# Fifteen of 32 experts in 64 rows with raw fp32 weights: one kernel for a transformer block with experts and a second block

## What is computed

```
def expert_block(args):
    xblk, e = args
    gu = xblk @ w_gate_up[e] + b_gate_up[e]
    gate = jnp.minimum(gu[:, :D_EXPERT], SWIGLU_LIMIT)
    up = jnp.clip(gu[:, D_EXPERT:], -SWIGLU_LIMIT, SWIGLU_LIMIT)
    act = gate * jax.nn.sigmoid(SWIGLU_ALPHA * gate) * (up + 1)
    return act @ w_down[e] + b_down[e]
```

## Time and profile before

| what | value |
|---|---|
| median of 3 runs | 1837.42 us (1836.15 to 1837.75) |
| the profiled execution's own time | 1836.11 us |
| its span | 1834.4 us |
| PE busy | 1756.2 us (96%) |
| DVE busy | 1517.9 us (83%) |
| ACT busy | 1148.2 us (63%) |
| POOL busy | 306.4 us (17%) |
| moved by DMA | 504.74 MB, 275 GB/s over the span |
| granted PE clock, mean | 0.98 |

### The profile page before, as it was taken

One profiled execution on the slowest core, in us unless ns is written; L12 is line 12 of the kernel. 1 busy time (PEld: TensorE's weight loads), 2 busy tenths in 40 slices (PEclk: granted clock), 3 DMA queues, 4 the chain that ended last, 5 costly groups with the idle time before them and its releaser, 6 DMA issues. The chain is left out here.

```text
span 1834.4 us, 25163 instructions
## 1 busy us (share of the span) xinstructions
PE 1756.2 (96%) x8429; PEld 1380.3 (75%) x8430; DVE 1517.9 (83%) x1693; ACT 1148.2 (63%) x1251; POOL 306.4 (17%) x331
## 2 busy tenths in 40 slices
PE   6988979999999999999999999999999799998998
PEld 3555457888888888888888888888886368887996
DVE  5366658999999999999999999999998657897663
ACT  5343316777777777777777777777774644436541
POOL 0140210121121121111112111111135100004420
PEclk9998969999999999999999999999999899999999
DMA  6032839999999999999999999999997522211001
GB/s 212 11 111 89 332 108 351 400 398 382 390 390 380 384 397 378 383 396 381 383 393 388 376 387 398 378 381 396 383 381 271 183 88 69 92 47 70 1 24 46
DMA packets 108519, 504.74 MB, mean 275 GB/s; under 512 B 22593, under 2 KB 40622, under 8 KB 58194
## 3 DMA queue, kind: packets, MB, share of 16 engines
q1 hardware_dynamic: 97314, 477.96, 67.6%
q0 software_dynamic: 11152, 26.10, 4.1%
HBM read 481.06 MB, written 22.95 MB: 275 GB/s over the span
## 5 line engine op out<-in xcount | busy, mean ns | idle before, releaser
L1776 DVE TENSOR_TENSOR part<-ring,part 128x2048 fp32r<-128x2048 f32 x258 | 584.4, 2286 | 35.5 <-ACT part L1474 35.5
L1474 ACT ACTIVATE part<-ring 128x2048 fp32r<-128x2048 f32 x256 | 486.4, 1921 | 135.2 <-PE bank L1627 75.4
L1604 PE MATMUL bank<-part,xT_hi 128*128 128x512 f32 x1536 | 390.8, 396 | 0.0
L1604 PEld LDWEIGHTS bank<-part,xT_hi 128*128 128x128 f32 x1536 | 281.4, 188 | 62.0 <-issue 7.3
L1474 ACT ACTIVATE part<-rest 128x2048 fp32r<-128x2048 f32 x124 | 238.2, 1922 | 96.4 <-PE bank L1604 70.9
L1776 DVE TENSOR_TENSOR part<-rest,part 128x2048 fp32r<-128x2048 f32 x124 | 281.3, 2292 | 0.0
L1638 PE MATMUL bank<-part,actT_hi 128*128 128x512 f32 x1024 | 277.0, 392 | 1.1 <-DVE part L1776 0.8
L1933 POOL DMA_INDIRECT rest<-h_rows,rest x33 | 88.1, 2671 | 944.9 <-PE bank L1587 928.6
L1638 PEld LDWEIGHTS bank<-part,actT_hi 128*128 128x128 f32 x1024 | 189.8, 188 | 39.5 <-issue 1.2
L1604 PE MATMUL bank<-part,xT_lo 128*128 128x512 f32 x768 | 205.9, 390 | 0.0
L1604 PEld LDWEIGHTS bank<-part,xT_lo 128*128 128x128 f32 x768 | 144.2, 188 | 31.4
(11 more groups left out here) (501 smaller groups left out, 2540.1 us busy)
## 6 DMA issues: line engine op xcount, KB each, us to landing
ring<-in_w_gate_up SPq DMA_DIRECT2D x194, 1024.0 KB, 7.8
ring<-in_w_down SPq DMA_DIRECT2D x66, 1024.0 KB, 6.8
rest<-in_w_gate_up SPq DMA_DIRECT2D x62, 1024.0 KB, 8.3
rest<-in_w_down SPq DMA_DIRECT2D x62, 1024.0 KB, 7.3
expert_rows<-rest SPq DMA_DIRECT2D x31, 512.0 KB, 8.4
ring<-in_w_in SPq DMA_DIRECT2D x14, 1024.0 KB, 5.2
rest<-in_w_ada SPq DMA_DIRECT2D x8, 1536.0 KB, 7.1
ring<-in_w_out SPq DMA_DIRECT2D x16, 512.0 KB, 5.9
```

The lines of the kernel that those rows point to most:

```text
L1474: nc.scalar.activation(hi[part(i, c)], raw(i, c), ACT.Copy).then_inc(sig("hi_ready"), counts)
L1604: ins = nc.tensor.matmul(bank[g][:], rows[:, c, :], w[:, g * 512:(g + 1) * 512], start=first, stop=last, skip_group_check=True)
L1776: V.tensor_tensor(lo[part(i, c)], raw(i, c), hi[part(i, c)].bitcast(F32), ALU.subtract).then_inc(sig("lo_ready"), counts)
```

## The change

The experts 1 to 30 are ranked by their number of rows when the router is done. The 15 with fewest take the odd turns ("small"), the other 15 the even turns ("big"); expert 0 stays first and 31 last. A small expert is computed for 64 rows. Its gathered rows are laid out in two halves: the partitions 0 to 63 hold the first half of the columns and 64 to 127 the second (`gather_small`, by rows of half the length). PE reads its raw fp32 chunks straight from the slots, with plain fp32 matmuls of 64 rows, two at a time by design: one writes to the partitions 0 to 63 of a bank, the other to 64 to 127 (the two column tiles). No high and low parts are made for it. Its activation is one 128 x 512 tile in place of two. Its slots come free when PE has used the chunk (`raw_used`). In a pair j, PE does gate and up of small expert j, down of the big one before, gate and up of the big one, down of the small one. The expert numbers are read by each engine from a table `order` that the first block makes; ranks, table and places of the results take new operations on DVE and three small matmuls on PE. An expert of the 15 with more than 64 rows would get an extra block.

The two projections use column tiles as well: the key rope's eight matmuls write to four groups of 32 partitions, and a matmul with `fold` adds them; the index keys' eight write to two groups of 64.

The diff, cut to its core:

```diff
+SMALL = 64
+PAIRS = 15
...
-            project(bank[4][64:96, :], w_in, D_IN1 - ROPE, ROPE)
+            for k in range(KT):
+                part = bank[4][32 * (k % 4):32 * (k % 4) + 32, :]
+                ins = nc.tensor.matmul(part, w_in[:, k, D_IN1 - ROPE:D_IN1], hT[:, k, :], start=(k < 4), stop=(k >= 4), skip_group_check=True)
+            ins.then_inc(sig("proj_done"), 1)
...
-            nc.tensor.matmul(bank[5][64:96, :], swap[64:96, :], k_rope[64:96, :], start=True, stop=True).then_inc(sig("k_swapped"), 1)
+            nc.tensor.matmul(bank[4][64:96, :], fold, k_rope, start=True, stop=True)
+            nc.tensor.matmul(bank[5][64:96, :], swap, k_rope, start=True, stop=True).then_inc(sig("k_swapped"), 1)
...
+            pe.wait_ge(sig("order_terms"), 1)
+            for n, by in enumerate((con(m, "token", 1, E - 1).broadcast_to([E - 1, P]), ones[0:E - 1, :], ones[0:E - 1, :])):
+                ins = nc.tensor.matmul(order_sum[:, n * E:(n + 1) * E], by, terms[0:E - 1, n * E:(n + 1) * E], start=True, stop=True, skip_group_check=True)
+            ins.then_inc(sig("ordered"), 1)
...
+            chain.link(V.scalar_tensor_tensor(out=key_row[0:E], in0=con(m, "iota", E, E), scalar=1.0 / 64, in1=count[0:E], op0=ALU.mult, op1=ALU.add))
+            chain.link(V.scalar_tensor_tensor(out=key_col[0:E], in0=con(m, "token", 1, E), scalar=1.0 / 64, in1=count_col, op0=ALU.mult, op1=ALU.add))
+            chain.link(V.tensor_scalar(under[0:E, 1:E - 1], key_row[0:E, 1:E - 1], key_col[0:E], 2.0, ALU.is_lt, ALU.mult))
+            chain.link(V.tensor_reduce(rank[0:E], under[0:E, 1:E - 1], AX, ALU.add))
...
+            dve.wait_ge(sig("ordered"), 1)
+            V.tensor_copy(f["order"][0:1], order_sum[0:1, 0:E])
...
+            chain.link(V.tensor_tensor(count[:, 1:E], count[:, 1:E], shift[:, 1:E], ALU.add))
             chain.link(V.tensor_scalar(extra, count, float(P), None, ALU.is_gt))
...
+            def store_small(j):
+                sp.wait_ge(sig("y_ready"), 2 * j + 4)
+                for g in range(2):
+                    sp.dma_start(m["y_dram"][bass.ds((P + SMALL) * j + P, SMALL), g * 512:(g + 1) * 512], y[g * SMALL:(g + 1) * SMALL, 0:512]).then_inc(sig("y_small_stored"), 16)
...
+            def rest_of_small(j, e, before):
                 for c in range(SLOTS, CHUNKS):
-                    wait_lo(sp, i, c - SLOTS)
-                    load_chunk(sp, a, m, i if c < 8 else i - 1, c, c % SLOTS)
+                    wait_raw(sp, j, c - SLOTS)
+                    load_chunk(sp, a, m, e if c < 8 else before, c, c % SLOTS)
...
+            with sp.Fori(0, PAIRS - 1) as j:
+                e1, e2 = (expert_at(sp, 2 * j + n) for n in (1, 2))
+                rest_of_big(j, e2, e1)
+                e3 = expert_at(sp, 2 * j + 3)
+                after_big(j, e3)
+                rest_of_small(j + 1, e3, e2)
+                after_small(j + 1, expert_at(sp, 2 * j + 4))
...
+            def gate_up_small(c, u):
+
+                w = raw_slot(m, c % SLOTS)
+                for h in range(2):
+                    ins = nc.tensor.matmul(bank[2 * u][h * SMALL:(h + 1) * SMALL, :], xT_small[:, c, :], w[:, (2 * u + h) * 512:(2 * u + h + 1) * 512], start=(c == 0), stop=(c == 7), skip_group_check=True)
+                return ins
...
+            def down_small(j, c):
+
+                pe.wait_ge(sig(f"chunk_loaded{c}"), 32 * j + 32)
+                w = raw_slot(m, c % SLOTS).rearrange("p (k n) -> p k n", k=2)
+                for k in range(2):
+                    n = 2 * (c - 8) + k
+                    for g in range(2):
+                        ins = nc.tensor.matmul(bank[6][g * SMALL:(g + 1) * SMALL, :], actT_small[:, n, :], w[:, k, g * 512:(g + 1) * 512], start=(n == 0), stop=(n == 7), skip_group_check=True)
+                ins.then_inc(sig("raw_used"), 1)
...
+            with pe.Fori(0, PAIRS - 1) as j:
+
+                small_turn(j)
+                big_gate_ups(j)
+                turn_rows_small(2 * j + 3)
+                pe.wait_ge(sig("index_ready"), 2 * j + 5)
+                big_down(j)
...
-            tile(1, w_small, 0, DI)
+            for k in range(KT):
+                ins = M.matmul(bank[1][64 * (k % 2):64 * (k % 2) + 64, :], w_small[:, k, 0:DI], hT[:, k, :], start=(k < 2), stop=(k >= KT - 2), skip_group_check=True)
+            ins.then_inc(sig("tile_done"), 1)
...
+            pe.wait_ge(sig("ik_parts_ready"), 1)
+            pe.wait_ge(sig("fold_ready"), 1)
+            M.matmul(bank[1][:], fold, ik_parts, start=True, stop=True).then_inc(sig("ik_folded"), 1)
```

More of the change, by code:

```diff
@@ L345, in first_block @@
     gsum, ginv = room.take(T), room.take(T)
+    key_row, under, terms = room.take(E), room.take(E), room.take(3 * E)
+    key_col, rank, small_e, at_e = (room.take(1) for _ in range(4))
+    order_sum = bank[4][:, (T + 2) * E:(T + 5) * E]
+    count_col = bank[4][0:E, (T + 1) * E:(T + 1) * E + 1]
     SCALE = QK ** -0.5
@@ L1285, in expert_places @@
     f["gate"], f["sigm"], f["up"], f["act"] = (keep.take(2, 512) for _ in range(4))
+    f["iota_small"], f["half"] = keep.take(P), keep.take(1)
     assert keep.at <= m["late_end"]
@@ new lines, in rest_of_big, with after_small @@
+            def rest_of_big(j, e, before):
+                for c in range(SLOTS, CHUNKS):
+                    wait_lo(sp, first(j) + 4 + c - SLOTS)
+                    load_chunk(sp, a, m, e if c < 8 else before, c, c % SLOTS)
+            def after_small(j, e, store=True):
+                for c in range(SLOTS):
+                    if c + SLOTS < 8:
+                        wait_raw(sp, j, c + SLOTS)
+                    else:
+                        wait_lo(sp, first(j) + c + SLOTS - 8)
+                    load_chunk(sp, a, m, e, c, c)
+                    if c == 0 and store:
+                        store_small(j - 1)
@@ L1529, in _ @@
-            make_hi(1, 3, 2, (0, 7))
-            make_hi(1, 4, 2, (0, 4))
-            make_hi(1, 5, 2, (0, 5))
-            with act.Fori(1, E - 1) as i:
-                turn(i)
-            i = E - 1
+            make_hi(2, 6 % RAW, "chunk_loaded6", 1, 2)
+            make_hi(3, 7 % RAW, "chunk_loaded7", 1, 3, counts=1 + 4)
+            sigmoid(7)
+            copy_rows_small(1)
+            with act.Fori(0, PAIRS - 1) as j:
+                small_turn(j)
+                for s in range(8, CHUNKS):
+                    hi_of_pair(j, s)
+                sigmoid(first(j) + 11)
+                copy_rows_small(2 * j + 3)
+                copy_y_small(j)
@@ L1536, in _ @@
+            j = PAIRS - 1
+            small_turn(j)
+            for s in range(8, CHUNKS):
+                hi_of_pair(j, s)
+            hi_of_last(0)
+            sigmoid(first(j) + 11)
+            hi_of_last(1)
+            copy_rows(E - 1, PAIRS + 2)
+            for c in (2, 3, 4):
+                hi_of_last(c)
+            copy_y_small(j)
+            hi_of_last(5)
             nc.scalar.activation(spare[0:1, 0:1], con(m, "ident", 1)[0:1], ACT.Sigmoid)
             for c in (6, 7):
-                make_hi(i, c, i + 1, (i, c - PARTS))
@@ L1704, in _ @@
-            i = E - 1
-            for h in range(2):
-                pe.wait_ge(sig(f"clipped{h}"), i)
-            gate_ups(i, i, more=False)
-            wait_actT(i)
-            pe.wait_ge(sig("y_ready"), i + 1)
+            first_gate_ups(0, (0, 1), 1)
+            for c in (2, 3):
+                gate_up(c, c, c)
+            biases(0)
+            gate_up(4, 4, 4)
+            list_next(0)
+            gate_up(5, 5, 5)
+            gate_up(6, 2, 6)
+            gate_up(7, 3, 7, counts=1 + 4)
@@ L1710, in _ @@
+            first_gate_ups(LAST, (0, 1), PAIRS + 2, [(f"act_ready{h}", PAIRS + 1) for h in range(2)])
+            turn_act(0, PAIRS + 1)
+            turn_act(1, PAIRS + 1)
+            for c in (2, 3):
+                gate_up(LAST + c, c, c)
+            biases(E - 1)
+            for c in (4, 5, 6, 7):
+                gate_up(LAST + c, c % PARTS, c)
+            wait_actT(PAIRS + 1)
+            pe.wait_ge(sig("y_ready"), E)
             for c in (8, 9, 10):
-                down(i, c)
+                down(LAST + c, c % PARTS, c)
@@ L1855, in _ @@
+            list_of(iota, expert_at(dve, 2))
+            index(2)
+            clip(7)
             gated(0)
-            rows_lo(2)
             times_gate(0)
+            with dve.Fori(0, PAIRS - 1) as j:
+                small_turn(j)
+                list_of(iota, expert_at(dve, 2 * j + 4))
+                for s in (6, 7, 8):
+                    lo_of_pair(j, s)
+                index(2 * j + 4)
+                for s in (9, 10, 11):
+                    lo_of_pair(j, s)
+                clip(first(j) + 11)
+                gated(j + 1)
+                times_gate(j + 1)
@@ L1858, in _ @@
+            j = PAIRS - 1
+            small_turn(j, last=True)
+            for s in range(6, CHUNKS):
+                lo_of_pair(j, s)
+            clip(first(j) + 11)
+            lo_of_last(0)
```

(9 more changed lines are left out.)

581 lines of the change are left out of this document (356 added, 225 removed).

## The result

The changed kernel takes **1846.57 us** (median of 5 runs, 1843.58 to 1849.50) against 1837.42 on the same chip: 1.005 times the kernel before, interval 1.0037 to 1.0063. It is 0.5% slower where I forecast 5% faster. The profiled execution took 1843.58 us, 1841.9 of it span.

What follows compares the result with a forecast made beforehand. PE bounds the loop now, DMA after the change; span 1834.4 - 90.9 + 3 + 3.4 - 2.3 - 3 = 1744.6 us, so 1746 us for an execution, about 5% faster, range 1708 to 1816.

Steps and rivals of the forecast that it cites:

- The view of the bound: Expert loop: PE sets the 35.33 us turn; after the change PE has 58.1 us a pair and DMA becomes the bound.
- Step 1: PE's small turn: 24 pairs of fp32 matmuls with column halves fully overlapping cost 21.0 us, replacing 32.6 us.
- rival B: Small gate-up and down on PE: column halves do not overlap, 79.1 us a pair, 1968 us; chance 0.10.
- C: Small turn on PE: halves overlap but weight loads do not, 71.3 us a pair, 1848 us; chance 0.03.
- Step 2: ACT and DVE in the loop: twelve copies and twelve subtractions a pair go; both then follow DMA, far under 60 us.
- step 3: DMA in the loop: mean 414 GB/s, 64.6 us a pair against 70.66, 90.9 us gained over fifteen pairs.
- PE's work at a low clock: After PE's idle at the end of each small gate-up: 1.5 to 2 us lost, covered by 6 us of slack.
- The mechanism that I gave for the thin queue: Big gate-ups: PE falls about 11 us behind DMA, small down chunks hold slots, queue thin for a quarter of the pair.
- Rival A: Loop: DMA cannot beat today's mean of 386 GB/s, 69.3 us a pair, 20 us gained, 1815 us; chance 0.12.
- Step 4: Order of experts: DVE waits for three small matmuls and does more operations before the first list, +3.4 us.
- Step 5: Projections in column tiles: key rope -2.3 us with two tiles at once, index keys -3 us.
- The last expert: Last expert: PE reaches its first two chunks while DMA is just ahead, about 3 us lost once.

Runs made afterwards that it cites:

- e11: e4 with both 64-row products of the small turn summed onto the same column half and bank half, so they cannot run side by side: 2002.73 us.
- e9: e4 without the loop's gathers of rows and gate-up bias loads, GpSimd signalling at once instead: 1757.94 us.
- e4: The changed kernel with the three moves of e1, e2 and e3 together: 1776.54 us, 0.9675 of the kernel before.
- e1: The changed kernel with DVE's copy of the big expert's index moved behind the last of the six subtractions: 1786.3 us.
- e12: The kernel before plus only the computing of the order of experts, results unread: 1841.52 us, against 1836.91 on its chip.
- e8: The kernel before plus only the two projections in column tiles with their folds: 1829.8 us, against 1837.0 on its chip.
- e3: The changed kernel with DVE's copy of the small expert's index put ahead of subtractions 0 and 1: 1837.57 us.
- e2: The changed kernel with ACT's copy of the big results put behind high parts 6 and 7: 1845.93 us.
- e7: e4 with ACT's small-activation copy behind high parts 8 and 9, list early, index copy behind subtraction 8, small down chunks spread between big gate-up chunks: 1780.38 us.

## Why the prediction was wrong, step by step

**The view of the bound** held as far as PE's work goes: 58.1 us of it a pair were left by my sum. The trace of the kernel after has 62.1 us busy, of which by my estimate 2.5 are the low clock behind the wait ahead of the down chunks (2.72 and 2.55 us where 1.37 follow) and 1.0 that behind the wait at chunk 5, so 58.6 without them.

**Step 1, PE's small turn, 21.0 us: right.** 3.65 us for 16 records show the halves side by side, and rivals B and C did not happen. e11 puts rival B's price at 2002.73 us where I had 1968, even on a kernel with the waits moved away: its pair is 82.0 us where I had 79.1.

**Steps 2 and 3 are what failed.** Step 2 says of ACT and DVE that "both follow DMA now". They can only where nothing in their queues waits for PE. In the kernel before the copy of the index never waited for the list (no such wait between 600 and 1100 us). The change takes work from PE, DVE and ACT, DVE gets ahead of PE, and the same kind of copy in the middle of its queue ties it to PE's pace again: 4.20 us, once a pair. I counted SP's table reads, the store and the gather among the new waits and priced them at zero; for the first two the trace bears me out as far as it shows. For the gather the zero is not shown: e9, without gathers and bias loads, is 19 us faster than e4, and their 3% of the bytes cannot be told from their waits there. DVE's and ACT's own queues I did not go through. That was the rule I should have used: where a change adds or moves a wait, name what is queued behind it.

In numbers: step 3's 64.6 us a pair was measured as 71.18. The wait for the list is worth 3.5 us a pair (e1; 53 us over fifteen pairs, where the medians have 60 for the whole kernel), the two other waits behind it another 1.1 (e4), and 2 us are left as told above. By PE's own account I had 58.1 us busy and 6.5 waiting, and it was 62.1 and 9.1: 2.6 us more waiting, which is the wait at chunk 5, and 4.0 more busy. So the larger part of the miss is PE's work at a low clock, which I gave 1.5 to 2 us a pair and had lie in slack. It cost 2.5 behind the wait ahead of the down chunks, which was 6.3 us on average and not 5 because the small index stood behind one subtraction more than I had counted, and another 1.0 behind the wait at chunk 5. None of the 2.5 lay in slack: between the down chunks and big chunk 5 PE has no wait in the timeline that could take it up.

The mechanism that I gave for the thin queue shows in e4, though shorter than my quarter of the pair: between 819 and 831 us, at the end of the big gate-up and the start of the small down, the windows have 371, 335, 427 and 154 GB/s, and elsewhere in the pair 394 or more. A pair with the waits for the list gone took 66.55 us, inside my own 62.2 to 68, and e4's 1776.54 us lies inside the range that I gave; the changed kernel's 1846.57 does not. **Rival A** is the one that e1 and e4 refute, with 396 and 403 GB/s as means of whole stretches.

**Step 4, the order of experts, +3.4: close.** e12 measures +4.6. DVE's wait for the sums is 4.07 us long, and its last operation of the block starts at 269.46 in e12's trace and at 265.88 in that of before, 3.6 us later; the remaining 1 us is no more than the interval of e12.

**Step 5, the projections, -2.3 and -3: the first mis-sized.** Together -7.2 us (e8; 3.9 to 8.4 by its interval). The index keys went from 7.08 to 3.65 us, as forecast. The key rope took the end that I had named, four at once, and not the two that I took: 1.92 us and not 3.9. My reason for two, that a matmul's two records must follow each other before the next tile can start, does not hold.

**The last expert, +3: close.** PE waits 1.44 and 2.46 us there. By the two traces the list of the first expert starts 0.7 us later than before (the order against the key rope), the stretch from there to the second block is 10.1 us longer, 7.8 of it in the loop and 2.3 at the loop's two ends, and the second block is 3.3 us shorter: 7.5 us, the difference of the spans. The medians differ by 9.15.

## What to carry to other kernels

When a change relieves the engine that sets the pace, go through the queue of each helper and mark every instruction that waits for that engine: a wait that was free while the helper ran behind it becomes the new bound as soon as the helper runs ahead, and everything queued behind it, down to the loads of the slots, goes at the old pace. Then ask what each such wait does to the pacing engine's clock. Put such instructions behind the work that frees buffers, or make what they wait for earlier; the one gave 60 us here, the other 58. And try it in combination: e3 alone was worth 9 us and e2 nothing while the larger wait stood.

## What the hardware showed that I had not expected

Plain fp32 matmuls in four column tiles of 32 overlap in full: 16 records in 1.92 us against 7.1 in one tile. The Trainium skill (TensorE: Matmul & The Clock Gate, Measured speedup vs the span model) has 2.38 times for three column tiles; here it is 1.94 times for two (7.08 against 3.65 us, e11) and 3.7 times for four.

A wait of PE can cost more than its length, and the length alone does not tell the cost. In e7, behind one of 2.30 us, four down matmuls took 1.20 us; in e4, behind one of 3.88, they took 2.07, and the window there shows a granted clock of 0.54, for the most part the 1.2 GHz level. But in e7 the window behind a wait of 2.34 us (at 789.15) has 0.51, in e4 four matmuls behind a wait of 3.65 took 1.20, and the waits of 2.57 us at chunk 5 in the kernel after were followed by full clock in three pairs of eight and by less in five. PE's timeline and a window of e7, then the same of e4:

```profile
855.11 1.20 PE L1826 MATMUL bank<-part,actT_hi 128*128 128x512 f32 x4 [2.30 <-DVE part L2031]
```
```profile
789.00:792.00 3.00, 2.85 (x7) 2.27 (x8) 2.60 (x3) 2.66 (x3) 3.00 (x5) 0.51 1.03 429
```
```profile
1119.10 1.20 PE L1823 MATMUL bank<-part,actT_hi 128*128 128x512 f32 x4 [3.65 <-DVE part L2023]
```
```profile
855.00:858.00 3.00, 3.00 (x9) 2.38 (x8) 2.81 (x2) 1.88 (x1) 0.00 (x0) 0.54 1.02 411
```

PE's busy time is thus no fixed number either: e4's 61.0 us a pair against my 58.1 hold such stretches.
